# A two-layer block with expert retrieval: the accumulation of the V rows on TensorE set three places behind the dots instead of four

## The reference, cut to what matters

```python
a = jnp.einsum('cd,ced->ce', xb, u_tab[eb])       # one dot per token and expert
w = (gb * jax.nn.gelu(a, approximate=False))
return jnp.einsum('ce,ced->cd', w, v_tab[eb])      # sum of V rows, weighted
```

## Time and profile before

| what | value |
|---|---|
| median of three runs | 3586.7 us |
| the profiled execution | 3566.7 us |
| its span, first to last instruction | 3565.2 us |
| TensorE busy | 2514.8 us, 71% |
| VectorE busy | 2381.3 us, 67% |
| ScalarE busy | 1369.1 us, 38% |
| GpSimd busy | 1112.4 us, 31% |
| bytes moved by DMA | 1343.61 MB, mean 377 GB/s |
| mean granted TensorE clock | 0.83 |

### The profile page before, as it was taken

The page is one execution under the profiler, slowest core; times in us unless marked ns, Lnnn a source line. Parts: engine busy times, 40 slices in busy tenths (PEclk is TensorE's granted clock), DMA queues, the critical chain, the costliest instruction groups (busy, mean ns, idle before and its releaser), DMA issues.

```text
span 3565.2 us, 40112 instructions
## 1 busy us (share of the span) xinstructions
PE 2514.8 (71%) x13640; PEld 977.5 (27%) x13640; DVE 2381.3 (67%) x5690; ACT 1369.1 (38%) x3647; POOL 1112.4 (31%) x1038
## 2 busy tenths in 40 slices
PE   7768669676696866966677777767676778855555
PEld 3432333222332223322222232222332233311111
DVE  7447873687836878377565786578675877566664
ACT  1113332344323443233373436434472438433222
POOL 0002332223322233232333333332432334343332
PEclk9788779797798977988778888988898889977766
DMA  7659899999999999999999999999999999999998
GB/s 242 227 200 381 350 354 407 416 406 397 361 402 416 416 388 364 411 387 399 385 415 386 388 396 403 395 386 415 382 394 393 399 388 400 380 386 378 376 371 336
DMA packets 228013, 1343.61 MB, mean 377 GB/s; under 512 B 28360, under 2 KB 33768, under 8 KB 95968
## 3 DMA queue, kind: packets, MB, share of 16 engines
q0 software_dynamic: 148320, 1076.50, 75.4%
q1 hardware_dynamic: 78816, 262.43, 19.2%
q10 hardware_dynamic: 672, 2.12, 0.1%
HBM read 1338.24 MB, written 2.71 MB: 376 GB/s over the span
## 4 chain that ended last, share of the span: by engine, by line
DMA 29%; PE 28%; DVE 18%; issue 14%; ACT 5%; POOL 4%; SPq 1%; POOLq 0%; ACTq 0%; DVEq 0%
DMA ring<-in_k_uv,idx 15%; PE ps L1537 13%; DMA ring<-in_k_vu,idx 11%; PE ps L1466 10%; DVE ring L372 7%; POOL ring L1938 4%; DMA wsl<-in_k_wu 4%; ACT L1122 2%; DVE big L420 1%; PE ps L1519 1%; PE ps L1675 1%; ACT diag L1122 1%; DVE rowB L420 1%; PE ps L1621 1%; ACT xr L1122 1%
## 5 line engine op out<-in xcount | busy, mean ns | idle before, releaser
L372 DVE CUSTOM_DVE_ANT_0 ring<-ring,xn 128x1024 f32<-128x1024 f32 x1024 | 1240.0, 1222 | 668.7 <-DMA ring<-in_k_uv,idx 372.4
L1466 PE MATMUL ps<-ring,diag 64*64 64x512 f32 x8192 | 1298.5, 757 | 532.3 <-ACT diag L1122 516.6
L1938 POOL DMA_INDIRECT ring<-in_k_vu,idx x512 | 549.1, 1072 | 1259.2 <-DVE aw L372 699.3
L1938 POOL DMA_INDIRECT ring<-in_k_uv,idx x512 | 557.2, 1088 | 1098.6 <-DVE aw L372 884.0
L1537 PE MATMUL ps<-wsl,xT 128*128 128x512 f32 (+1 forms) x1536 | 729.3, 621 | 73.6 <-DMA wsl<-in_k_wu 48.7
L1466 PEld LDWEIGHTS ps<-ring,diag 64*64 64x64 f32 x8192 | 312.2, 161 | 1273.7 <-ACT diag L1122 766.5
L1122 ACT ACTIVATE aw<-aw 128x2 f32<-128x2 f32 x512 | 104.0, 203 | 1322.8 <-DVE aw L372 1321.6
L1122 ACT ACT_TABLE_LOAD x374 | 479.8, 1283 | 71.9 <-DVE big L420 59.7
L1537 PEld LDWEIGHTS ps<-wsl,xT 128*128 128x128 f32 x1536 | 292.2, 200 | 526.4 <-issue 441.3
L1122 ACT ACTIVATE diag<-gid,aw 128x64 f32<-128x64 f32 x1024 | 305.8, 341 | 110.4 <-PE ps L1466 93.7
L1122 ACT ACTIVATE gid<-ident,gate 128x64 f32<-128x64 f32 x1024 | 292.5, 332 | 0.0
(11 more groups left out here) (227 smaller groups left out, 2020.6 us busy)
## 6 DMA issues: line engine op xcount, KB each, us to landing
wsl<-in_k_wu SPq DMA_DIRECT2D x408, 512.0 KB, 10.6
wsl<-in_k_wmod SPq DMA_DIRECT2D x48, 512.0 KB, 13.3
ring<-in_k_vu,idx POOLq DMA_INDIRECT x512
ring<-in_k_uv,idx POOLq DMA_INDIRECT x512
wsl<-in_k_wu SPq DMA_DIRECT2D x16, 280.0 KB, 18.9
big<-in_b_gate SPq DMA_DIRECT2D x4, 1024.0 KB, 11.1
big<-in_conv_w SPq DMA_DIRECT2D x4, 768.0 KB, 22.3
hres<-in_x SPq DMA_DIRECT2D x4, 512.0 KB, 6.7
```

Source lines behind the costliest of these rows:

```text
L372: V(v.tensor_tensor_reduce(u_row(s), u_row(s), xn[:, b, :], 1.0, 0.0, ALU.mult, ALU.add, aw[:, b, k:k + 1]), ("dot", s))
L1466: r = t.matmul(PA[half][64 * q:64 * q + 64, :], diag[64 * half:64 * half + 64, s % (2 * PAIR), :], v_row(s)[64 * half:64 * half + 64, 512 ...
L1938: Q(p.indirect_dma_start(out=both_rows(s), out_offset=None, in_=tab, in_offset=bass.IndirectOffsetOnAxis(ap=idx[:, n % 2, k:k + 1], axis=0 ...
```

## The change

The constant VL goes from 4 to 3. In TensorE's program `vmm(s)` stands at slot s + 3 in place of s + 4. The slots of `evacuate`, `permute`, `finish` and `finish2` on ScalarE, TensorE and VectorE, which are counted from VL, move one slot earlier too, and the last slot number END = NSLOT + VL + 6 is one less. Nothing is added or removed.

```diff
@@ -19,7 +19,7 @@
 NWS = 6
 NSLOT = 1024
 PAIR = 2
-VL = 4
+VL = 3
 END = NSLOT + VL + 6
```

## The result

The changed kernel takes 3623.9 us (median of four runs, 3619.1 to 3637.7), the kernel before 3584.7 (four runs). The ratio is 1.0117, with a 95% interval of 1.0086 to 1.0148: **slower by 1.2%**. The forecast was 3582 us, no change, and the range ended at 3617. The medians are only 39 us apart, because the traced execution of the kernel before was 18 us under its median and the one after at its median.

A forecast was written before the change was run, and what follows sets the result against it. The DMA engines were taken to bound the kernel. Gain -53, ring +46 and the rest +2 made -5 us against the profiled execution, applied to the median of 3586.7: 3582 us, 8-in-10 range 3546 to 3617.

The forecast's parts named there:

- the gain: V moves ahead of woven blocks: 46 us in layer 1's `mid1`, 7 at slot 35; 53 us, bounds 20 to 73.
- the ring: `att2` steps 1 to 9, after odd slots: scores wait for diagonals behind the previous exponential; 46 us, bounds 10 to 89.
- What bounds the kernel: Whole kernel: it lives off the DMA engines (queues fill 94.6%); a change pays only where they starve.
- rival 4: Table load on ScalarE within the ring: the switch costs more than its instruction shows; chance 0.02, slower.
- the clock term: TensorE in the ring: waiting costs it its clock, 1.4 us on three in ten of 36 turns, 15 us.
- pass 4 changes little: `att2` in pass 4: rows are shorter, the ring is about 4.8 us and costs nothing.
- a wait of 2 us costs the engines nothing visible: `mid1`: the next V's gather waits 2 us more than its dot, harmless with three gathers in flight.
- those after 9 stay at 5: `att2` in pass 7: steps after 9 stay 5 us apart, while steps 1 to 9 are 6 to 8.
- what costs nothing: Other odd positions, weight buffers and the moved end of the sums: 2 us for all, bounds 0 and 15.
- Rival 2: Ring at half clock in `att2` steps 1 to 9: 76 us against 43 of gain, +33, 3620 us; chance 0.22.
- Rival 1: `att2`: the ring doesn't close or is short; gain 53, cost 10, 3544 us; chance 0.25.
- rival 3: Where TensorE is ahead, V waits for its diagonal at any position, so nothing changes: 3586 us; chance 0.10.

The follow-up runs named there:

- experiment 1: Changed kernel, but V four slots behind its dot again in slots 44 to 81 of layer 2's attention passes: 3562.2 us, 0.9927 of the kernel before.
- Experiment 7: experiment 1 with V two behind in the slot ahead of each woven block in layer 1's `mid1` stretches: 3535.4 us, 0.9882 of the kernel before.
- experiment 9: Changed kernel with ScalarE making the pair's diagonals ahead of the exponential in layer 2's attention steps: 3571.3 us, 0.9946 of the kernel before.
- 3: Changed kernel with layer 2's attention shifted one slot later, so steps 1 to 9 begin after even slots: 3594.0 us, 1.0026 of the kernel before.
- experiment 5: Changed kernel plus ten unused identity matmuls on TensorE in steps 3 to 10 of layer 2's attention: 3619.6 us, 1.0123 of the kernel before.
- experiment 2: Kernel before (V four behind) with V three behind only in slots 44 to 81 of layer 2's attention passes: 3651.1 us, 1.0206 of the kernel before.
- experiment 6: Changed kernel with the end of the sums (`evacuate`, `permute`, `finish`) left in its old slots: 3625.5 us, 1.0142 of the kernel before.
- 10: experiment 9 with V two behind in the slot ahead of each woven block of layer 1: 3559.4 us, 0.9909 of the kernel before.
- 11: Kernel before with V two behind only in the slot ahead of each woven block of layer 1: 3554.2 us, 0.9888 of the kernel before.
- 8: Kernel before plus the same ten filler matmuls as experiment 5: 3598.5 us, 1.0056 of the kernel before.

## Why the prediction was wrong

The forecast was -53 for the gain, +46 for the ring and +2 for the rest. The two traces give about -30, +61 and +25, which is their 56 us. The 61 us between forecast and traces are 23 of gain that did not come, 15 of clock in the ring, 15 in the slots behind the ring and 8 in slots 80 to 88.

**What bounds the kernel**: right. Both the gain and the loss showed as a DMA rate, and each repair that fed the engines made the kernel faster: 415 GB/s in pass 7 and a ratio of 0.9927 in experiment 1, 404 GB/s in layer 1 and 0.9882 in 7, 392 GB/s in pass 7 and 0.9946 in 9.

**The ring**: right in place, in every link, in parity (3) and in the way that it runs (9), and at full clock in length: 4.94 us from L1007 to V as read, and 5.67, 6.43 and 7.12 us for the longer turns of passes 5, 6 and 7 (experiment 5), where the forecast had means of 5.5 and 6.1 and a longer turn of 7.1. The 31 us of the sum stand; by all turns of experiment 5 at the full clock they would be 34 at most. The table load cost in the ring what its instruction shows: it starts at 3027.26, 0.03 us behind the instruction before it, and gelu starts at 3028.55, 0.01 us behind the load. In all nine turns from 2986 to 3059 us gelu starts 0.01 us behind its load. The 0.02 of rival 4 in the chances stood for a switch that costs ScalarE more than its instruction shows; no run shows such a cost, and what the trace shows is the load of 1.28 us alone.

**First step that failed: the clock term, "1.4 us on three in ten of 36 turns, 15 us".** Measured are 61.4 - 31 = 30 us. The price of a turn was about right (1.1 to 1.8 us from pass 4 to pass 7, 1.5 in the mean, for 1.4); the share was not. With 1.00 and 0.50 as the levels of the trace, a granted clock of 0.57, 0.72, 0.67 and 0.66 means full speed for (0.57 - 0.5)/0.5 = 14%, 44%, 34% and 32% of the time, so some seven in ten at the half clock. The prediction took three in ten, and its case against more was that TensorE pauses only 2 us at a time in the ring. That was an argument without a row; the pauses in pass 7 were 0.4 to 2.5 us long, and the granted clock was 0.66 all the same. The row that I had, 0.76 to 0.80 at pauses of 7 us, says 40 to 48% of the time at the half clock, already more than three in ten.

**Second: "pass 4 changes little".** It lost 9.5 us. At the full clock its ring is as long as two gathers (4.8 us forecast, 5.01 in experiment 5), but without slack; at the half clock it is 6.02 and 6.19, and there it stayed from the third turn to the ninth, in the changed kernel and in experiments 2 and 6. A ring that costs nothing at the full clock (5.01 us) had to be priced at the half clock too (6.02 and 6.19).

**Third: the gain, "a wait of 2 us costs the engines nothing visible", three quarters of 61.6 us and 7 at slot 35.** Layer 1 gave 31.0 us in its three stretches and 27.3 by the start of layer 2, slot 35 some 3 (slots 30 to 46 of its three passes: 131.9 us before, 129.0 after). The rates stayed under the 395 GB/s that I had named. Experiment 7 removes just that wait and the rate goes to 404: it was the wait, not VectorE. POOL's waits for V ended at 284 us, not under 150, mostly because those outside `mid1` stay: the three stretches hold 50 us of them, and held 89 before. The forecast of the second gather itself was exact, 2 us behind its dot; that it costs nothing was a guess. That a POOL wait is harmless while three gathers are in flight has a row only for waits on the dot at the undisturbed rate: from 1070 to 1150 us of the kernel before, POOL waited 44.5 of 80 us for dots, at 416 GB/s.

**Fourth: "those after 9 stay at 5".** Slots 64 to 80 took 14.7 us more, at a clock of 0.84 in pass 7, and its steps from 9 to 15 took 36.3 us in place of 28.7. It is not the lag there: experiment 2 has the same lag in these slots and takes 0.8 us more. What it goes with is the clock at which the ring leaves TensorE. The first interval behind the ring, from step 9 to step 10, with its granted clock, and what slots 64 to 80 took over the kernel before:

| trace | pass 4 | pass 5 | pass 6 | pass 7 |
|---|---|---|---|---|
| before | 2.49 us at 0.5 | 2.49 at 1.0 | 2.91 at 1.0 | 3.31 at 1.0 |
| the change | 3.37 at 0.5: +2.2 | 4.43 at 0.5: +2.3 | 5.49 at 0.5: +3.5 | 6.56 at 0.5: +6.7 |
| experiment 2 | 3.36 at 0.5: +1.4 | 2.45 at 1.0: -0.9 | 2.95 at 1.0: -0.1 | 3.50 at 1.0: +0.4 |
| experiment 6 | 3.36 at 0.5: +0.8 | 2.45 at 1.0: -0.1 | 5.49 at 0.5: +4.4 | 6.56 at 0.5: +6.3 |

In the eight cases where this interval ran at the half clock the slots took 0.8 to 6.7 us more, in the four where it ran at the full one 0.9 less to 0.4 more. No edit of mine set this clock, so that it is the cause is not shown. At which level a ring ended differed between traces of nearly the same program, so another execution may show less of these 15 us. Where no ring closes, the slots take 5.0 and 3.4 us more with a lag of 3 (experiments 9 and 10) and 5.4 and 4.5 with a lag of 4 there (7 and 11).

The 10.2 us of slots 80 to 88 go with a lag of 3 there. In the seven traces that have it without the shift (the change and experiments 1, 5, 6, 7, 9 and 10) these slots take 3.4 to 12.8 us more than before, in the three with a lag of 4 (2, 8 and 11) 0.8 to 2.6. The prediction had put this place under "what costs nothing", with 2 us for all and 15 as the bound; what waits there I did not look into.

**Rivals.** Rival 2, slower by the ring at half clock, was the case: mechanism, place and condition hold (the mean turn was 6.87 us, past its 6.5), and its 3620 us came within 4 us (+33 forecast, +39 measured). In part that is luck: it had 76 for the ring and 43 of gain, measured are 61 in its place, 25 behind it, and some 27 to 30 of gain. It deserved more than 0.22: the only argument against it was the length of the pauses. Rival 1 (no ring) and rival 3 (nothing happens) fell, by the timeline and by experiments 1 and 2, which show both parts at full size. The end of the sums at no cost was right (6).

## What to carry to other kernels

Before a consumer is moved one place earlier in a hand-woven order, ask in what groups its input is made and what the producer's program has ahead of that group: with pairs, half of the positions are free and the other half tie the consumer to the producer's next wait. Where the gain comes from a few places, move it there alone (twelve slots gave 1.1%, as much by the medians as any other variant), and where a ring threatens, reorder the producer (one line in experiment 9). Price every chain through TensorE at both clock levels that the trace shows (here V of a slot took 1.09 and 1.98 us, the scores of a step 1.12 and 2.07), and a ring that is only just as long as the pace as if it ran at the slower one (here 5.01 and 6.02 to 6.19 us in pass 4, at a pace of 4.98).

## What the runs showed that I had not expected

**A ring can keep the clock low while TensorE looks busy.** In these busy times slow matmuls count in full: V's eight take 1.98 us at 0.50, and 1.09 at the full clock. TensorE was busy 60.6 of 73 us in pass 7, 83%, with six pauses over 0.3 us, of 0.4 to 2.5 us, and was granted 0.66; before, it was busy 40.0 of 47 us, 85%, with twelve pauses of 0.3 to 1.2 us, and was granted 0.96. The turns at the half clock (8.49 and 8.96 us) are a slow version of the same chain, and adding 2.45 us of idle work per turn made them shorter (6.64 and 7.12 us, at a granted clock of 1.0, experiment 5). The profile's busy time was no guide to the clock: 83% stood beside 0.66, and 85% beside 0.96.

**A filler is not free.** Ten small multiplications a step cost 0.56% alone (8): in passes 6 and 7, where TensorE has least room, it came to work without a pause and slots 46 to 64 took 50.4 and 53.9 us in place of 47.3 and 47.1.
